# Attention on one Trainium2 core: ScalarE copies a step's first transposed probabilities ahead of the exponentials of two steps on

## The reference, cut to what matters

```
a: p = softmax(q k' / 8) per pair of half heads;  y = (p[0] - lam * p[1]) @ v     (8 heads)
b: p = softmax over keys and a sink, windowed mask;  y = p @ v                    (16 query heads, 4 kv heads)
c: p = softmax(qn kn' + qr kr');  y = p @ v                                       (8 heads)
merged = sum over the three of sigmoid(gate) * (y @ branch_w);  out = merged @ w_out
```

## The kernel before, in words

| engine | first half of step s | second half of step s |
|---|---|---|
| PE | turn(s, 0), L927 | scores(s+3), turn(s, 1) in b and c, turn_output in a, weighted(s-1) |
| DVE | normalize(s+1), squares and factor in a | biases(s+3): maximum of the scores |
| ACT | output, **copy(s, 0)**, output_high | copy(s, 1) in b and c, inverse and back in a, **exp(s+3)** |

## Time and profile before

### The profile page before, as it was taken

One profiled execution on the slowest core, in us unless ns is written; L12 is line 12 of the kernel. 1 busy time (PEld: TensorE's weight loads), 2 busy tenths in 40 slices (PEclk: granted clock), 3 DMA queues, 4 the chain that ended last, 5 costly groups with the idle time before them and its releaser, 6 DMA issues.

```text
span 2785.6 us, 42026 instructions
## 1 busy us (share of the span) xinstructions
PE 2698.2 (97%) x15406; PEld 2259.9 (81%) x15406; DVE 1743.5 (63%) x2891; ACT 1244.0 (45%) x2212; POOL 218.9 (8%) x302
## 2 busy tenths in 40 slices
PE   8999999999999999999999999999999989998998
PEld 6888898876666776788888898888988777868996
DVE  7777376666755443358676385773677886645764
ACT  3222355236555434445222353222553576555543
POOL 0000010110100000011010000010102110000000
PEclk9999999999999999999999999999999999999999
DMA  7555356421111221145455455553555322425654
GB/s 282 180 198 184 99 175 224 145 86 39 46 46 39 69 84 49 53 152 182 165 191 167 118 173 177 193 191 109 158 186 176 118 76 69 125 76 159 226 181 152
DMA packets 105634, 384.42 MB, mean 138 GB/s; under 512 B 12049, under 2 KB 12321, under 8 KB 103569
## 3 DMA queue, kind: packets, MB, share of 16 engines
q1 hardware_dynamic: 85250, 303.34, 33.8%
q0 software_dynamic: 20240, 79.14, 8.7%
HBM read 379.27 MB, written 3.16 MB: 137 GB/s over the span
## 4 chain that ended last, share of the span: by engine, by line
PE 85%; DVE 9%; ACT 3%; DMA 1%; issue 1%; POOL 0%; SPq 0%; DVEq 0%; ACTq 0%; POOLq 0%
PE ps L2187 22%; PE ps L2195 22%; PE ps L2188 22%; PE ps L957 3%; PE ps L936 3%; DVE wlo L1614 2%; PE ps L919 2%; PE ps L2251 1%; PE ps L2253 1%; PE ps L2248 1%; PE ps L909 1%; DVE mx L807 1%; ACT prob L723 1%; PE ps L2127 1%; PE ps L2278 1%
## 5 line engine op out<-in xcount | busy, mean ns | idle before, releaser
L1614 DVE TENSOR_TENSOR wlo<-raw,whi 128x1024 fp32r<-128x1024 f32 x570 | 696.1, 1229 | 425.4 <-ACT whi L1234 424.5
L2187 PE MATMUL ps<-xhi,whi 128*128 128x512 f32 (+1 forms) x2432 | 820.8, 352 | 6.1 <-DVE xlo L1805 5.3
L1234 ACT ACTIVATE whi<-raw 128x1024 fp32r<-128x1024 f32 x570 | 602.8, 1058 | 501.4 <-PE ps L2195 411.5
L2188 PE MATMUL ps<-xlo,whi 128*128 128x512 f32 (+1 forms) x2432 | 813.5, 349 | 0.0
L2187 PEld LDWEIGHTS ps<-xhi,whi 128*128 128x128 f32 x2432 | 462.5, 190 | 70.6 <-DVE xlo L1805 6.5
L2188 PEld LDWEIGHTS ps<-xlo,whi 128*128 128x128 f32 x2432 | 462.6, 190 | 57.4
L2195 PE MATMUL ps<-xhi,wlo 128*128 128x512 f32 (+1 forms) x2432 | 505.4, 350 | 2.5 <-DVE wlo L1614 2.5
L2195 PEld LDWEIGHTS ps<-xhi,wlo 128*128 128x128 f32 x2432 | 399.4, 190 | 60.5 <-DVE wlo L1614 3.1
L1944 DVE SCALAR_TENSOR_TENSOR work<-ada,work 128x1024 f32<-128x1024 f32 x256 | 299.4, 1220 | 5.9 <-DMA ada<-in_ada_rows 5.9
L807 DVE TENSOR_REDUCE mx<-ps 128x2 f32<-128x1024 f32 (+1 forms) x120 | 125.2, 1045 | 196.1 <-PE ps L915 81.9
L2187 PE MATMUL ps<-ghi,whi 128*128 128x256 f32 (+1 forms) x792 | 233.5, 320 | 0.1
(11 more groups left out here) (253 smaller groups left out, 3394.5 us busy)
## 6 DMA issues: line engine op xcount, KB each, us to landing
raw<-in_ffn_in SPq DMA_DIRECT2D x192, 512.0 KB, 4.7
ada<-in_ada_rows POOLq DMA_DIRECT2D x128, 512.0 KB, 4.0
raw<-in_merge SPq DMA_DIRECT2D x96, 512.0 KB, 3.4
raw<-in_ffn_out SPq DMA_DIRECT2D x72, 512.0 KB, 3.5
raw<-in_v_a SPq DMA_DIRECT2D x32, 512.0 KB, 4.2
raw<-in_qk_a SPq DMA_DIRECT2D x32, 512.0 KB, 3.5
raw<-in_ffn_out SPq DMA_DIRECT2D x36, 384.0 KB, 3.1
raw<-in_out_rows SPq DMA_DIRECT2D x22, 512.0 KB, 4.4
```

The source lines that it names most:

```text
L1234: act.activation(whi[:, g.ring(SPLIT), :], raw[:, g.ring(RAW), :], ACT.Copy).then_inc(hi_ready, 1)
L1614: dve.tensor_tensor(wlo[:, g.ring(SPLIT), :], raw[:, g.ring(RAW), :], whi[:, g.ring(SPLIT), :].bitcast(F32), ALU.subtract).then_inc(lo_rea ...
L2187: pe.matmul(o, w, hi[:, first + c, ph.span], start=start, stop=False)
L2188: pe.matmul(o, w, lo[:, first + c, ph.span], start=False, stop=False)
```

## The change

ACT's exponentials move. Before, exp(s+3) stood at the end of step s, behind copy(s, 1), inverse and back, and ahead of the second tick of the step, the next output and copy(s+1, 0). Now it stands in the first half of step s+1, right behind copy(s+1, 0), written there as exp(s+2) of the step itself. The exp(2) ahead of the loop goes into step 0 in the same way. No instruction is added or taken away; PE, DVE, GpSimd and the DMA queues keep their order.

```diff
             exp(0)
             exp(1)
             yield
-            exp(2)
             for s in range(ph.steps):
                 for b in ended(ph, s - 2):
                     output(b)
                 if s < len(units):
                     turned_copy(s, 0)
+                if s + 2 < len(units):
+                    exp(s + 2)
                 if ph.mode != "b":
                     for b in ended(ph, s - (6 if ph.mode == "a" else 3)):
                         output_high(b)
...
                     for b in ended(ph, s - 5):
                         back(b)
-                if s + 3 < len(units):
-                    exp(s + 3)
                 yield
```

## The result

The changed kernel took **2769.52 us** (median of 5 executions, 2766.08 to 2770.81), against 2784.97 us before (now 5 executions, 2782.69 to 2791.33). The ratio is 0.9941, with a 95% interval of 0.9931 to 0.9952: faster by 15.5 us, where 15 were forecast. The profiled execution took 2770.81 us, over a span of 2769.1 at a mean granted clock of 0.993.

The account below looks back on a forecast made before the run. PE bounds the kernel, busy 2698.2 of 2785.6 us, so only its waits could be won. Terms summed to 18.1 us, less a sixth 15, from the median 2784.97 to 2770 us; range 2763 to 2781.

Parts of the forecast that it names:

- two signs of being wrong: PE's L732 waits fall by less than half, or they fall and the six attentions still take 648 us.
- The clock's terms: Starts of b0 and b1: with less idle time PE's granted clock holds, 3.5 us of the gain.
- a sixth taken off: Taken off the 18.1 us sum, giving 15: part of a gain would end as PE waits for DVE's normalize.
- Turn(s, 1) in b0: Middle of b0: with the copy ahead of the exp, scores cover it and three stalls go; gain 3.5 us.
- the new waits: exp(s+2) ahead of copy(s, 1), inverse and back delays PE, mainly in steps 15, 19, 24 of b0; loss 1.8 us.
- the start of b0: First turns of b0: copy(0, 0) ahead of exp(2) gains 3.4 us, 1.4 without the clock.
- The starts: First turns of b0 and b1, copy ahead of exp(2): gains of 3.4 and 4.3 us, clock included.
- The new wait of back: In a, back stands behind exp(s+2): 0.1 us lost in two steps.
- Consumers of the exp: DVE's normalize, turn and scores meet a later exp; taken as no loss, bound 0.68 us at a normalize.
- Rival 1: DVE takes over: PE waits for normalize instead, only the starts gain, 5.7 us, 2779 us; chance 0.15.
- Rival 2: Single bank TURN is the limit: each exp delays some copy, gain nothing, 2785 us; chance 0.08.
- Rival 3: Exp ahead of copy(s, 1) costs 0.9 us in 34 steps of b and c: 13 us slower, 2798; chance 0.07.

Follow-up runs that it names:

- E5: Kernel before, with exp(s+2) at the end of step s where exp(s+3) stood, and no exp(2) ahead of the loop: 2774.97 us, ratio 0.9959.
- E1: Kernel before, with only exp(2) moved behind copy(0, 0) in each of the six attentions: 2777.12 us, ratio 0.9971.
- E6: The change, but with exp(2) left ahead of the loop: 2778.92 us, ratio 0.997 to the kernel before.
- E3: Kernel before, with the change made in a alone, b and c as before: 2779.33 us, ratio 0.9979.
- E7: The change, with back put ahead of inverse in a: 2771.27 us, ratio 0.9947 to the kernel before.
- E9: The change, with the exp behind copy(s, 1) in narrow steps without a tick (15, 19, 24 in b0): 2766.91 us, ratio 0.9928 to before.
- E10: The change itself, unaltered, run once more beside the kernel before: 2768.24 us, ratio 0.9934.

## Why the prediction was right, point by point

**The mechanism** holds in b's and a's turns. The checks that the prediction named came out: the stalls of rows 4 and 5 are gone (of the 1.21 us at 624.71 there are 0.69 left, for DVE's `prob`), turn(0, 1) of b1 follows its scores, the granted clock there is 1.00, PE's wait for `tmp` at turn(16, 0) has come, and ACT's idle time ahead of L723 and L721 fell from 82 to 19 us. But one of its two signs of being wrong came out as well: the turns' waits for L732 were to fall by half or more, and they fell by 44% (17.8 to 9.9 us). The sign was badly drawn. It left out the turn_outputs, which wait for the same copies under the name "issue"; with them the fall is 55% (23.6 to 10.6). And it counted waits that the forecast itself kept or added: `turned_c` (3.8, now 3.5), the next turn at both starts (0.92 and 0.99), the two new ones of 0.68. The other sign did not: the stretches of a and b are 20.5 us shorter.

E5 says more than the prediction did. It spoke of the exp *ahead of the copy*; an exp with its input ready may stand there and costs far less. Of the two things the change does, the later unit (ready input) carries most: alone it gives 11.5 us in time, and in the stretches of a and b 9.1 of the 13.2 us of standing still. The change's place, behind the copy and half a step earlier, gives the rest.

**The sum, split.** The terms without the clock make 14.6 us, and 13.2 us of standing still went. The clock's terms make 3.5 us, and 7.3 us of busy time went. So the waits were a little under what was forecast and the clock's part was the **term that was mis-sized**: it came out twice as large. That the total came within 0.5 us of 15 is in part luck: more clock than forecast, less from the waits, and a sixth taken off for a reason that did not come true.

**Turn(s, 1) in b0 and the new waits** (3.5 - 1.8), with the start of b0 (3.4) and a small one at 898.89: b0 to c0 fell by 7.6 us where about 5.5 were forecast. By the windows 4.2 of these are waits, where the terms without the clock make about 3.5, and 3.4 are busy time, where the clock's share was 2.0. The new waits were 0.68 us at step 15 (0.9 forecast) and 0.68 at step 19 (0.35). At step 24 the wait of turn(25, 0) rose from 0.19 to 0.28 us (0.35 forecast). In step 29 there are no scores at all, where the prediction had wide ones to hide the exp; no new wait came there even so.

**The starts.** b1 to c1 fell by 5.3 us where 4.3 were forecast, and E1 gave 8.9 for the starts of all six attentions, where the terms 3.4 and 4.3 make 7.7. In b1 the waits gave 2.5 us (2.8 forecast) and the busy time 2.8 (1.5 forecast).

**The clock's part** (3.5 us of those) came in the change, larger than forecast, but is less certain than the waits. The same pair of stalls at the start of b0, 1.69 and 0.78 us, is in E6 and in E3. In E6 both turns and the lo half behind them ran slow, as before; in E3 they did not, and b0 to c0 took 280.4 us there against 283.1, with as much standing still (timeline, the turns and the lo half of E6, then those of E3):

```profile
779.53 1.05 PE L936 MATMUL ps<-ident,prob 128*128 128x128 f32 x4 [1.69 <-ACT turned_b L732]
...
781.36 1.09 PE L936 MATMUL ps<-ident,prob 128*128 128x128 f32 x4 [0.78 <-ACT turned_b L732]
...
782.10 3.76 PE L2195 MATMUL ps<-yahi,wlo 128*128 128x512 f32 x8
```

```profile
777.70 0.63 PE L940 MATMUL ps<-ident,prob 128*128 128x128 f32 x4 [1.69 <-ACT turned_b L732]
...
779.10 0.63 PE L940 MATMUL ps<-ident,prob 128*128 128x128 f32 x4 [0.78 <-DVE prob L838]
...
779.49 2.07 PE L2199 MATMUL ps<-yahi,wlo 128*128 128x512 f32 x8
```

**a.** a0 to b0 fell by 6.0 us, of which some 1.6 are a stretch at 1.2 GHz at the end of a0 (the mean granted clock from 760 to 780 us was 0.91) that is absent after (1.00); nothing in the prediction spoke of it. It is absent in E1 too (1.00), where of a's exponentials only exp(2) was moved, so the change of the steady steps need not be what removes it. In a1 the forecast was 3.3 us (1.84 less 0.1, 1.16, and the share of 2255.52), and 1.6 came (2.1 of waits). That is the other term that was mis-sized. The new wait of back was put at 0.1 us in two steps, and it is 0.70 and 0.92, since not exp(s+2) but `inverse`, blocked on DVE's `ysum`, holds it. E7 shows that putting back first doesn't win it: the wait goes to GpSimd's and ACT's outputs.

**Consumers of the exp** at nothing, and **c**, which had no term: c0 to a1 gave 1.3 us, and c1 nothing. PE has no new wait for normalize in b0 (the 0.55 at 885.02 is gone too).

**The sixth taken off** was the right size for another reason. The stretches of a and b gained 20.5 us in the two traces, more than the 18.1 of the sum. Between those traces 3.6 + 1.7 us went at the front and at the end, and the whole differs by 16.5. The front varies by 3.9 us between executions (615.6 to 619.5) with no change of the work there, by its granted clock. No pile of waits for `prob` took anything back, which the prediction gave as the reason.

**The rivals.** Rival 1, DVE takes over: PE's waits for normalize (`prob`) came to 2.0 us before (1.4 and 0.6 by line) and to 1.1 after; they fell. (Its price of 5.7 us took b1's 4.3 as waits, though 1.5 of them were the clock's; 4.2 would have been its own sum.) Rival 2, the bank `TURN` is the limit: it forecast no gain. The Trainium skill (Perfetto Trace Analysis, Matmuls) asks for rotating banks there. Order alone brought 15.5 us with the single bank, and E9 some more, so the bank was not what most of these waits were for. Whether a second bank would bring as much or more was not tried, and no run here speaks against that rule itself. Rival 3, slower by the exp ahead of copy(s, 1): its price was paid in two steps of b0, and a tenth of a microsecond in a third (E9 took it back), not in 34.

## What to carry to other kernels

On an engine that works in order, look for an instruction that waits for its input, or starts late because of it, while one behind it is waited for. Put it later, until its input is old, before thinking of its length or of more buffers; the same work at the same place in the queue gave 11.5 us once its input was ready. Then see what the later place holds up, since each reader also frees a buffer (E5's scores). The stalls where a pipeline fills can be worth as much as all the steady ones together (8.9 against 7.5 us here, a part of both by the clock): read the first two steps of each stage by themselves. And split a gain into standing still and busy time before you credit it to waits: here a third of what the stretches of a and b gained was busy time.

## What the runs showed of the hardware

The granted clock did not follow PE's stalls alone. At the start of b0, with stalls of 1.69 and 0.78 us, the ten microseconds around ran at a granted clock of 0.66 before and in E6, and at 1.00 in E3. Windows of E6, then of E3:

```profile
778.00:788.00 10.00, 7.69 (x28) 5.11 (x28) 4.88 (x13) 4.10 (x13) 0.00 (x0) 0.66 0.17 54
```


```profile
776.00:786.00 10.00, 7.53 (x52) 5.42 (x51) 7.05 (x19) 6.08 (x19) 0.00 (x0) 1.00 0.17 54
```

The lo half alone differs by 1.7 us (3.76 against 2.07). E3 and E6 are different versions, so this does not tell whether the order of a or the execution decides.

The front of the kernel tells more, since its instructions are the same in every version. From 20 to 60 us PE shows no idle time at all (as far as the modelled ends of its matmuls tell), and still the clock fell for a part of it, and not for the same part each time. Windows of before, then of after:

```profile
20.00:60.00 40.00, 40.00 (x177) 31.92 (x176) 32.02 (x73) 18.73 (x31) 6.01 (x12) 0.83 0.73 275
```

```profile
20.00:60.00 40.00, 40.00 (x161) 32.09 (x160) 28.39 (x67) 17.20 (x29) 5.99 (x11) 0.74 0.72 273
```

The same changed kernel had 0.74 in one execution and 0.79 in another (E10), and its front took 619.4 and 617.0 us. So some microseconds of this kernel come and go between executions by the clock. What decides it stays open.
